# Turning the expert hidden rows on VectorE, from one quarter of the partitions into another, instead of on TensorE

## The reference

```
aff = softmax(xf @ w_router)                 # 1024 tokens x 16 experts
gate, idx = top_k(aff.T, cap)                # cap = 128 tokens for each expert
xe = xf[idx]
hid = silu(xe @ w_gate[e]) * (xe @ w_up[e])  # 128 x 1024, for each expert and group
ye = (hid @ w_down[e]) * gate
y.at[idx].add(ye)
```

## Time and profile before

| | |
|---|---|
| median of 3 runs | 2404.12 us (2403.29 to 2409.57) |
| span of the profiled execution | 2402.6 us |
| the profiled execution's own time | not listed apart; the runs' median is 1.5 us above its span |
| TensorE busy | 2296.1 us, 96% |
| VectorE busy | 1208.7 us, 50% |
| ScalarE busy | 1103.8 us, 46% |
| GpSimd busy | 603.2 us, 25% |
| expert stage | about 1285 to 2390 us, 16 experts, 68.9 us each |

### The profile page before, as it was taken

How to read it: one execution, slowest core, us unless ns; L and a number is a source line. 1 busy time by engine, 2 the same in 40 slices (tenths; PEclk the granted TensorE clock), 3 DMA queues, 4 the chain that set the end, 5 groups by cost and what they waited for, 6 DMA issues and landing times. The chain is left out here.

```text
span 2402.6 us, 35196 instructions
## 1 busy us (share of the span) xinstructions
PE 2296.1 (96%) x13583; PEld 1915.1 (80%) x13583; DVE 1208.7 (50%) x1881; ACT 1103.8 (46%) x1828; POOL 603.2 (25%) x676
## 2 busy tenths in 40 slices
PE   6999999999999999999947999999999999999997
PEld 4679989777899897667736888888888888888886
DVE  3222334554413346665566555544445556666655
ACT  4223444655433436665543444444444455555552
POOL 3004342443133324430021011111110122222434
PEclk9999999999999999999978999999999999999999
DMA  8835445658454459764547566666666678888785
GB/s 319 259 107 182 145 160 185 191 150 185 122 194 141 162 177 249 228 180 158 170 189 263 204 211 221 214 226 210 207 203 231 216 268 309 322 308 291 284 302 175
DMA packets 239040, 511.49 MB, mean 213 GB/s; under 512 B 36981, under 2 KB 128005, under 8 KB 235825
## 3 DMA queue, kind: packets, MB, share of 16 engines
q1 hardware_dynamic: 190960, 394.78, 49.0%
q0 software_dynamic: 47936, 114.77, 16.0%
HBM read 415.32 MB, written 93.69 MB: 212 GB/s over the span
## 5 line engine op out<-in xcount | busy, mean ns | idle before, releaser
L2492 DVE TENSOR_TENSOR moe_w_lo<-moe_wf,moe_w_hi 128x2048 fp32r<-128x2048 f32 x192 | 439.5, 2292 | 456.6 <-ACT moe_w_hi L2367 450.0
L2367 ACT ACTIVATE moe_w_hi<-moe_wf 128x2048 fp32r<-128x2048 f32 x192 | 367.8, 1916 | 551.4 <-PE moe_acc L2630 550.5
L2630 PE MATMUL moe_acc<-moe_w_hi,moe_x_hi 128*128 128x512 f32 x1024 | 401.7, 392 | 0.9 <-DVE moe_x_lo L2498 0.6
L2630 PE MATMUL moe_acc<-moe_w_hi,moe_x_lo 128*128 128x512 f32 x1024 | 398.9, 390 | 0.0
L2630 PE MATMUL moe_acc<-moe_w_lo,moe_x_hi 128*128 128x512 f32 x1024 | 398.4, 389 | 0.0
L2630 PEld LDWEIGHTS moe_acc<-moe_w_hi,moe_x_hi 128*128 128x128 f32 x1024 | 192.3, 188 | 40.7 <-DVE moe_x_lo L2498 0.8
L2630 PEld LDWEIGHTS moe_acc<-moe_w_hi,moe_x_lo 128*128 128x128 f32 x1024 | 192.2, 188 | 40.3
L2630 PEld LDWEIGHTS moe_acc<-moe_w_lo,moe_x_hi 128*128 128x128 f32 x1024 | 192.4, 188 | 38.9
L1793 PE MATMUL banks<-fr_w_hi,fr_h_hi 128*128 128x256 f32 x768 | 223.2, 291 | 0.0
L1793 PE MATMUL banks<-fr_w_lo,fr_h_hi 128*128 128x256 f32 x768 | 217.0, 283 | 0.0
L1793 PE MATMUL banks<-fr_w_hi,fr_h_lo 128*128 128x256 f32 x768 | 216.9, 282 | 0.0
(11 more groups left out here) (294 smaller groups left out, 4083.4 us busy)
## 6 DMA issues: line engine op xcount, KB each, us to landing
moe_wf<-in_w_expert_gate SPq DMA_DIRECT2D x64, 1024.0 KB, 4.9
moe_wf<-in_w_expert_up SPq DMA_DIRECT2D x64, 1024.0 KB, 4.9
moe_wf<-in_w_expert_down SPq DMA_DIRECT2D x64, 1024.0 KB, 5.8
fr_w_raw<-in_w_units SPq DMA_DIRECT2D x28, 1024.0 KB, 7.2
fr_bias<-in_na_bias SPq DMA_DIRECT2D x16, 1520.0 KB, 11.1
fr_a_w<-in_w_ada POOLq DMA_DIRECT2D x16, 1024.0 KB, 9.0
scratch_qk_t<-fr_stage SPq DMA_DIRECT2D x64, 256.0 KB, 2.5
scratch_vov<-fr_stage SPq DMA_DIRECT2D x96, 128.0 KB, 2.2
```

The costliest lines, as they stand in the source:

```text
L2367: nc.scalar.activation(w_hi[:, q, :, :], wf[:, q, :, :], ACT.Copy).then_inc(w_hi_ready, 1)
L2492: nc.vector.tensor_tensor(w_lo[:, q, :, :], wf[:, q, :, :], w_hi[:, q, :, :].bitcast(F32), ALU.subtract).then_inc(w_lo_ready, 1)
L2630: mm = nc.tensor.matmul(acc[:, j, b, :], x[:, g, k, :], w[:, q, a, h * HALF:(h + 1) * HALF], start=(k == 0 and i == 0), stop=(k == KC - 1 ...
```

## The change

For every expert but the last, hid is turned by VectorE. A transpose of VectorE turns blocks of 32x32. One instruction takes 32 tokens (partitions t * 32 and on) and 256 hidden columns (the quarter u), and writes 32 partitions of quarter u: partition u * 32 + c gets the columns u * 256 + q * 64 + c * 2 + a, for q = 0..3 and a = 0, 1. 4 x 4 instructions for each group, 32 for each expert. So the hidden columns stand on the partitions in another order, and the rows of w_down are loaded in that order (`by_quarter`). The result goes to `h_raw`, which lies in the place of `h_lo`; ScalarE makes h_hi from it and VectorE h_lo in place, one instruction for each group.

VectorE's order becomes: split of GATE(e+1) pieces 0 to 2, multiply, split of GATE piece 3, drain, the 32 transposes, split of DOWN(e) piece 0, h_lo, split of DOWN piece 1 and the rest. ScalarE's h_hi stands after its split of DOWN piece 0. TensorE makes the four pieces of GATE(e+1) in one go, waits for h, and goes on to DOWN(e). The last expert stays as it was, with semaphores of its own. SyncE's loop over the first eight experts is unrolled.

```diff
+    QT = P // 4
+    by_chunk = [w.rearrange("e (q a p) n -> e q p a n", p=P, a=PIECE) for w in weights]
+    by_quarter = [w.rearrange("e (u q c a) n -> e q u c a n", u=4, q=NP, c=QT) for w in weights]
+        with nc.sbuf_tensor("moe_h_raw", [P, GROUPS, KC, P], F32) as h_raw:
+            pass
         h_lo = s.sb("h_lo", [P, GROUPS, KC, P], F32R)
@@ SyncE
-                    sp.dma_start(wf[:, q, :, :], mats[step][e, q]).then_inc(w_loaded[q], 16)
+                    rows = by_quarter[step] if step == DOWN and e < NE - 1 else by_chunk[step]
+                    sp.dma_start(wf[:, q, :, :], rows[e, q]).then_inc(w_loaded[q], 16)
-            over_experts(sp, body)
+            for e in range(NE):
+                body(e, e % 2)
@@ ScalarE
+            def h_out(e):
+                for g in range(GROUPS):
+                    act.wait_ge(h_turned, ONE + e * GROUPS + g + 1)
+                    nc.scalar.activation(h_hi[:, g, :, :], h_raw[:, g, :, :], ACT.Copy).then_inc(h_hi_ready, 1)
                     split(e, DOWN, range(0, 1))
+                    h_out(e)
                     for n in ns[0:2]:
                         square(n)
-                    split(e, DOWN, range(1, 2))
-                    turned_out(e, (h_hi, j), h_turned, h_hi_ready)
-                    split(e, DOWN, range(2, NP))
+                    split(e, DOWN, range(1, NP))
@@ VectorE
+            def turn_h(e):
+                for g in range(GROUPS):
+                    for t in range(4):
+                        for u in range(4):
+                            columns = hid[t * QT:(t + 1) * QT, g, u * 2 * P:(u + 1) * 2 * P].rearrange("r (q c a) -> r q a c", c=QT, a=PIECE)
+                            turned = h_raw[u * QT:(u + 1) * QT, g, :, t * QT:(t + 1) * QT]
+                            a = nc.vector.transpose(turned, columns)
+                    a.then_inc(h_turned, 1)
+            def h_out(e):
+                for g in range(GROUPS):
+                    dve.wait_ge(h_hi_ready, ONE + e * GROUPS + g + 1)
+                    nc.vector.tensor_tensor(h_lo[:, g, :, :], h_raw[:, g, :, :], h_hi[:, g, :, :].bitcast(F32),
+                                            ALU.subtract).then_inc(h_ready, 1)
-                    split(e + 1, GATE, range(2, NP))
+                    split(e + 1, GATE, range(2, 3))
                     multiply(e, j)
+                    split(e + 1, GATE, range(3, NP))
+                    dve.drain()
+                    turn_h(e)
                     split(e, DOWN, range(0, 1))
+                    h_out(e)
                     for n in ns[0:2]:
                         mean(n)
                     split(e, DOWN, range(1, 2))
-                    turned_out(e, h_hi, h_lo, j, h_hi_ready, h_ready)
@@ TensorE
                     pe.wait_ge(x_ready, ONE + e * BK + 2 * BK)
-                    products(e + 1, GATE, 1 - j, x_hi[:, 1 - j], x_lo[:, 1 - j], first)
-                    turn_h(e, j)
-                    products(e + 1, GATE, 1 - j, x_hi[:, 1 - j], x_lo[:, 1 - j], second)
-                    pe.wait_ge(h_ready, ONE + e * BK + BK)
+                    products(e + 1, GATE, 1 - j, x_hi[:, 1 - j], x_lo[:, 1 - j])
+                    pe.wait_ge(h_ready, ONE + (e + 1) * GROUPS)
                     products(e, DOWN, j, h_hi, h_lo)
```

More of the change, by code:

```diff
@@ L2114, in experts @@
     mod_row = io["mod"].rearrange("g (m n) -> g m n", n=D)
-    mats = [io[f"w_expert_{n}"].rearrange("e (q a p) n -> e q p a n", p=P, a=PIECE) for n in ("gate", "up", "down")]
+    QT = P // 4
+    weights = [io[f"w_expert_{n}"] for n in ("gate", "up", "down")]
+    by_chunk = [w.rearrange("e (q a p) n -> e q p a n", p=P, a=PIECE) for w in weights]
+    by_quarter = [w.rearrange("e (u q c a) n -> e q u c a n", u=4, q=NP, c=QT) for w in weights]
     with ExitStack() as ctx:
@@ L2171, in experts @@
         hid_ready = s.sem("hid_ready")
+        last_h_turned, last_h_hi_ready, last_h_ready = (s.sem(f"last_h_{n}") for n in ("turned", "hi_ready", "ready"))
         h_turned = s.sem("h_turned")
@@ L2381, in silu @@
                 if len(bs) == BK:
-                    act.wait_ge(h_turned, ONE + e * BK)
+                    act.wait_ge(h_turned, ONE + e * GROUPS)
                 for b in bs:
@@ L2425, in body @@
                     split(e, DOWN, range(0, 2))
-                    turned_out(e, (h_hi, j), h_turned, h_hi_ready, range(0, 2))
+                    turned_out(0, (h_hi, j), last_h_turned, last_h_hi_ready, range(0, 2))
                     split(e, DOWN, range(2, NP))
@@ L2429, in body @@
                         square(n)
-                    turned_out(e, (h_hi, j), h_turned, h_hi_ready, range(2, BK))
+                    turned_out(0, (h_hi, j), last_h_turned, last_h_hi_ready, range(2, BK))
                 else:
@@ L2547, in body @@
                     split(e, DOWN, range(0, 2))
-                    turned_out(e, h_hi, h_lo, j, h_hi_ready, h_ready, range(0, 2))
+                    turned_out(0, h_hi, h_lo, j, last_h_hi_ready, last_h_ready, range(0, 2))
                     multiply(e, j, range(2, BK))
@@ L2552, in body @@
                         mean(n)
-                    turned_out(e, h_hi, h_lo, j, h_hi_ready, h_ready, range(2, BK))
+                    turned_out(0, h_hi, h_lo, j, last_h_hi_ready, last_h_ready, range(2, BK))
                     for n in ns:
@@ L2650, in turn_h @@
                 pe.wait_ge(hid_ready, ONE + e * BK + bs[-1] + 1)
-                turn(hid, j, h_turned, bs)
+                turn(hid, j, last_h_turned, bs)
             bs = [range(2 * g, 2 * g + 2) for g in range(GROUPS)]
@@ L2675, in body @@
                     products(e, UP, j, x_hi[:, j], x_lo[:, j], second, bs[1])
-                    pe.wait_ge(h_ready, ONE + e * BK + 2)
+                    pe.wait_ge(last_h_ready, ONE + 2)
                     products(e, DOWN, j, h_hi, h_lo, first, bs[0])
@@ L2679, in body @@
                     products(e, DOWN, j, h_hi, h_lo, second, bs[0])
-                    pe.wait_ge(h_ready, ONE + e * BK + BK)
+                    pe.wait_ge(last_h_ready, ONE + BK)
                     for b in bs[1]:
```

## The result

The changed kernel takes 2736.24 us (median of 4 runs, 2726.09 to 2740.43) for 2403.82 before: a ratio of 1.137, 95% interval 1.135 to 1.140. It is slower by 332 us. The prediction had the side right and the size wrong: 2424 us, at most 2500.

The account below looks back on a forecast made before the run. TensorE's issue rate bounds the expert stage. Each of 15 experts saves 1.78 us of transposes but adds 3.11 us of wait and restart, +1.33 each, +20 us: 2404 + 20 = 2424 us, range 2377 to 2500.

Parts of the forecast that it names:

- What bounds the kernel; the gain of 26.7 us: Expert stage runs at TensorE's issue rate; dropping 16 transposes in 15 experts saves 15 x 1.78 = 26.7 us at most.
- DOWN's weights in another row order have the same bytes, and w_hi waits for TensorE's release, not for a load.: Hidden edit in DOWN's loads: the new row order was expected to cost nothing.
- No wait for a load: Sign named for the profile after: no engine waits for a load; another wait than h_lo ahead of DOWN would refute.
- The transposes' duration: VectorE, 32 transposes an expert: 0.47 us each with the gap, 15.0 us in all; this duration decides the sign.
- slow transposes: Rival, chance 0.20: reading two words apart makes VectorE transposes take 0.6 to 0.73 us, giving 2487 to 2550 us.
- The changed quarter: VectorE: a transpose writing another quarter starts only after the last has ended, gap 0.02 to 0.05 us, without overlap.
- The chain and its wait: VectorE's queue from UP's end to h_lo: DOWN may start at 1425.75, GATE(e+1) ends at 1422.89, TensorE waits 2.86 us.
- The clock: Rival, chance 0.08: each expert's wait of 3 us lowers TensorE's clock, 1.5 us each, 22 us more: 2446 us.
- The windows, "half a microsecond over": Six experts with windows: DOWN2 is split at about 10.4 us after DOWN's start, wanted at 10.9, so covered.

Follow-up runs that it names:

- e8: As e11, but each VectorE transpose takes both groups (32 x 512), 16 instructions an expert in place of 32: 2387.2 us, ratio 0.9935 to the kernel before.
- e12: As e8, but in expert 14 alone all four pieces of UP(15) are split before the window's last two rows: 2387.2 us, ratio 0.993 to the kernel before.
- e2: Kernel before, SyncE's loop unrolled, with only DOWN's rows loaded by quarters for all experts but the last: 2739.4 us, ratio 1.140.
- e10: Kernel before, loop unrolled, with DOWN's rows loaded by sixteenths, 16 entries in the load's outermost dimension: 2449 us (one run).
- e11: As e7, with the two groups innermost in the transpose loop, so every second transpose stays in the same quarters: 2396.4 us, ratio 0.9971 to the kernel before.
- e3: Changed kernel with DOWN's rows loaded in the old order, leaving the VectorE transposes alone: 2437.9 us, ratio 1.0149 to the kernel before.
- e7: Changed kernel, transposes picking columns k * 128 + u * 32 + c, so DOWN's rows load in the old order: 2438.1 us, ratio 1.0144 to the kernel before.
- e9: As e7, with 19 identity transposes on TensorE filling its wait for h: 2425.2 us, ratio 1.009 to the kernel before.
- e4: Changed kernel, partition p taking columns p * 8 to p * 8 + 7; load 128 partitions outermost, transposes at step 8: 2555.6 us, ratio 1.064 to the kernel before.

## Why the prediction was wrong, step by step

- **What bounds the kernel; the gain of 26.7 us.** Right. In `e8` only 0.7 us of waits for h_lo are left, and an expert takes 67.07 us for 68.85: 1.78 less, as forecast. It is 15.9 us faster, and its one late wait with the low clock behind it would be some 14 more, 30 in all for 26.7 (an estimate); but in `e12`, without that wait, another came in its place.
- **"DOWN's weights in another row order have the same bytes, and w_hi waits for TensorE's release, not for a load."** This step failed, and it carries the loss: `e2`, with this edit alone, is 337 us slower. The bytes were the same and the load's shape was not; I priced the transfer by its size and took the 4.9 us of rows 11 and the slack of the wait for granted, so this term stood in the sum at nothing. The loads of before took 5.8 us to land with 128 partitions outermost. With 4 quarters outermost they come 12 to 15 us apart, where TensorE uses a piece in 5.44: the four packets in flight, 0.41 us each, make 128 x 0.41 / 4 = 13 us a piece (an estimate). The sign named for it, "No wait for a load", failed by 556.0 us, and TensorE waited 209.7 us for w_lo, which the sum didn't have. The Trainium skill (DMA: Bandwidth & Descriptors, section Why a DMA increments its semaphore by 16 and not by 1) says that a load uses the largest number of engines, up to 16, that divides the slowest dimension of both its sides; 4 here. The packets agree: 4, 8 and 16 in flight for 4, 8 and 16 entries. It should have been a rival: a quarter of the engines would have made the load alone about four times as long. The rule is not all of it: with 16 entries (`e10`) the loss is still 46 us.
- **The transposes' duration.** 0.47 forecast, 0.436 and a gap of 0.015 measured. A step of two words cost nothing; the rival "slow transposes" fell for step 2 and holds for step 8. Of the two rules of the Trainium skill named there, the note on cachelines in SBUF — State Buffer agrees (a step of two words is free), and the rule of adjacent pairs in Vector Engine (DVE) Microarchitecture Reference, section Measured stream behaviour on trn2, does not hold for this instruction: 0.436 us at step 1 and at step 2.
- **The changed quarter.** Right: 0.451 for changed quarters, and `e11`'s 12.41 us for the overlap where they stay.
- **The chain and its wait.** 2.86 us forecast, 2.19 measured in `e3` and `e7`; of the difference, 0.67, the transposes are 32 x 0.019 = 0.61.
- **The clock.** It stood as a rival with 0.08 and was true: a wait of 2.2 us was enough in ten experts of fifteen, at 1.6 us each where 1.5 was named, and `e9` puts it at 12.9 us. Rows 12 showed full clock in a stretch of short gaps, which was no evidence for one whole gap amid dense work.
- **The windows, "half a microsecond over".** Right where it was counted: no wait for DOWN's w_lo is left in `e7`. Not counted were the other two rows of a window, ahead of the last splits of UP(e+1). In expert 14 they wait for their own loads, and TensorE 8.1 us for them.
- So without the failed step the forecast would have been 2424 for 2438, and that it comes so near is in part luck: 15 waits shorter by 0.67 us (-10), the clock (+13) and expert 14 (+11) add up to the 14 us.

## What to carry to other kernels

When an edit reorders a load, compare its outermost dimension with the old one before its bytes: 4 where 128 stood cost 337 us here, and other columns for the transposes needed no new order at all. The number of packets on the profile's page changes with it, and the new order cost most where other loads ran beside it. When work moves onto an engine that feeds the bound one, add up its chain to the deadline, and count a wait of 2 us on TensorE as longer than it looks. Join short operations that change the quarter: 16 transposes of 512 took 11.45 us, 32 of 256 took 14.4.

## What the runs showed of the hardware that was not expected

- VectorE's transposes of 4-byte data took 0.703 us for 512 elements a partition and 0.436 for 256: 1.04 ns an element, as a tensor_tensor of the kernel before, and 0.17 fixed. With the columns 8 words apart 256 took 0.651; 2 words apart cost nothing.
- A transpose that changed the quarter followed the last after 0.451 us; one that didn't, after 0.326 (`e11`).
- 1 MB loads ran with as many packets in flight as their outermost dimension has entries: at most 4, 8 and 16, for 94 to 98% of the time. Without other loads beside them 8 were enough here (68.85 us an expert, as before). In the windows they were not (87.6), and neither were 16 (75.8).
- An 8 KB packet took 0.41 us with 4 in flight (`e2`) and 0.54 with 16 (`e10`), from rows by quarters and by sixteenths; 0.35 with 16, from rows 8 a partition (`e4`).
- TensorE's clock fell to its lower level, 1.2 GHz, behind ten of fifteen waits of 2.2 us in the midst of dense matmuls. It stayed up behind the ten shorter ones of `e11`.
